# A depthwise convolution split between TensorE and VectorE: 28 of 31 taps on TensorE in place of 24

## What is computed

```python
def conv_module(h, hist, w_pw1, b_pw1, w_dw, b_dw, g_ln, b_ln, w_pw2, b_pw2):
    a = h @ w_pw1 + b_pw1
    u = a[..., :D_MODEL] * jax.nn.sigmoid(a[..., D_MODEL:])
    ext = jnp.concatenate([hist.astype(u.dtype), u], axis=1)
    v = lax.conv_general_dilated(ext, w_dw[:, None, :], (1,), 'VALID',
                                 dimension_numbers=('NWC', 'WIO', 'NWC'),
                                 feature_group_count=D_MODEL) + b_dw
    v = layernorm(v, g_ln, b_ln)
    y = jax.nn.silu(v) @ w_pw2 + b_pw2
    return y, ext[:, -(CONV_WIDTH - 1):]
```

## Time and profile before

| | us |
|---|---|
| median of 3 runs | 1411.05 |
| lowest, highest | 1407.11, 1412.43 |
| the profiled execution | 1407.91 |
| its span in the trace | 1406.1 |
| PE, DVE, ACT, POOL busy | 1358.3, 841.4, 600.8, 728.6 |

### The profile page before, as it was taken

How to read it: one execution, slowest core, us unless ns; L and a number is a source line. 1 busy time by engine, 2 the same in 40 slices (tenths; PEclk the granted TensorE clock), 3 DMA queues, 4 the chain that set the end, 5 groups by cost and what they waited for, 6 DMA issues and landing times.

```text
span 1406.1 us, 26287 instructions
## 1 busy us (share of the span) xinstructions
PE 1358.3 (97%) x11038; PEld 1265.2 (90%) x11038; DVE 841.4 (60%) x1246; ACT 600.8 (43%) x1016; POOL 728.6 (52%) x505
## 2 busy tenths in 40 slices
PE   7899989999999999999999999999999999999997
PEld 7776589999999999999899867768999999999997
DVE  6999666755464544667565665554575454545434
ACT  5112254544444443445555644442364344443432
POOL 3333114488788876333322353430447788887831
PEclk9999979999999999999999999999999999999998
DMA  5443402233322223422111386761222332222221
GB/s 216 136 123 105 149 20 74 88 96 103 103 91 90 91 91 136 150 79 82 46 35 53 123 316 258 275 251 39 66 85 94 104 103 92 90 91 91 90 90 64
DMA packets 106196, 157.52 MB, mean 112 GB/s; under 512 B 7456, under 2 KB 91808, under 8 KB 100832
## 3 DMA queue, kind: packets, MB, share of 16 engines
q1 hardware_dynamic: 98528, 113.35, 25.4%
q0 software_dynamic: 7168, 41.95, 8.0%
q10 hardware_dynamic: 384, 0.55, 0.2%
HBM read 143.07 MB, written 4.03 MB: 105 GB/s over the span
## 4 chain that ended last, share of the span: by engine, by line
PE 85%; DVE 11%; ACT 1%; issue 1%; POOL 1%; DMA 0%; DVEq 0%; SPq 0%; ACTq 0%
PE ps L1627 28%; PE ps L1758 20%; PE ps L1746 18%; PE ps L1888 5%; PE ps L1928 3%; DVE v L1131 3%; PE ps L1977 2%; DVE tap L1118 2%; PE ps L1666 1%; ACT wh L713 1%; PE ps L1679 1%; PE ps L1958 1%; DVE v L1121 1%; POOL wl L573 1%; PE ps L1968 0%
## 5 line engine op out<-in xcount | busy, mean ns | idle before, releaser
L573 POOL TENSOR_TENSOR wl<-raw,wh 128x512 fp32r<-128x512 f32 (+2 forms) x252 | 439.6, 1746 | 475.3 <-ACT wh L713 475.1
L713 ACT ACTIVATE wh<-raw 128x512 fp32r<-128x512 f32 (+2 forms) x253 | 192.6, 762 | 373.5 <-PE ps L1627 190.8
L1627 PE MATMUL ps<-xh,wh 128*128 128x272 f32 x704 | 150.6, 296 | 22.0 <-DVE xl L1059 10.1
L573 POOL TENSOR_TENSOR wl<-wuv,wh 128x512 fp32r<-128x512 f32 x104 | 135.0, 1310 | 49.7 <-ACT wh L713 49.7
L1758 PE MATMUL ps<-mh,wh 128*128 128x272 f32 x768 | 158.6, 288 | 0.0
L1758 PE MATMUL ps<-mh,wl 128*128 128x272 f32 x768 | 158.6, 288 | 0.0
L1758 PE MATMUL ps<-ml,wh 128*128 128x272 f32 x768 | 158.3, 288 | 0.0
L1627 PE MATMUL ps<-xh,wl 128*128 128x272 f32 x704 | 147.6, 292 | 0.0
L1627 PE MATMUL ps<-xl,wh 128*128 128x272 f32 x704 | 147.6, 292 | 0.0
L1627 PEld LDWEIGHTS ps<-xh,wh 128*128 128x128 f32 x704 | 112.8, 193 | 27.3 <-POOL wl L573 15.0
L1758 PEld LDWEIGHTS ps<-ml,wh 128*128 128x128 f32 x768 | 120.4, 188 | 0.0
(11 more groups left out here) (307 smaller groups left out, 3026.0 us busy)
## 6 DMA issues: line engine op xcount, KB each, us to landing
raw<-w_up SPq DMA_DIRECT2D x32, 1024.0 KB, 5.5
raw<-w_down SPq DMA_DIRECT2D x32, 1024.0 KB, 5.2
raw<-w_pw SPq DMA_DIRECT2D x11, 1024.0 KB, 5.2
shifted<-ext SPq DMA_DIRECT2D x112, 66.5 KB, 2.0
raw<-w_o SPq DMA_DIRECT2D x4, 1024.0 KB, 5.5
raw<-w_dq SPq DMA_DIRECT2D x3, 1024.0 KB, 5.3
raw<-w_uq SPq DMA_DIRECT2D x4, 768.0 KB, 4.4
x<-xT SPq DMA_DIRECT2D x4, 544.0 KB, 7.6
```

The costliest lines, as they stand in the source:

```text
L573: pf.tensor_tensor(weight(wl, u), weight_raw(u), f32(weight(wh, u)), ALU.subtract).then_inc(w_lo, 1)
L713: af.activation(weight(wh, u), weight_raw(u), ACT.Copy).then_inc(w_hi, 1)
L1627: m = tf.matmul(ps[:, bank_of(u) + bank, 0:width], w[:, k, :], a[:, k, part], start=(k == 0 and n == 0), stop=(k == nk - 1 and n == 2))
```

## The change

One constant: the taps of the prompt's convolution that TensorE takes in chunks 0 to 6.

```diff
-PE_TAPS = 24
+PE_TAPS = 28
```

## The result

The changed kernel takes 1402.61 us (median of 7 runs, 1398.68 to 1405.43) against 1407.59 us for the kernel before beside it (7 runs). The ratio is 0.995, interval [0.993, 0.997], which is 7.0 us of 1408: it goes with the means of the same runs, 1401.67 and 1408.72 us, while the medians lie 5.0 us apart. Two more sets of runs on other occasions gave 0.9956 [0.9941, 0.9972] and 0.9952 [0.9935, 0.9969]. The profiled execution took 1402.61 us, its span is 1400.8 against 1406.1, so 5.3 us less. The forecast was 1403.9 us and a gain of 7.1 us, with the faster and the same case at nearly even chances, since it lay on the line of 0.5%. The measured ratio lies on that line too.

The account below looks back on a forecast made before the run. VectorE was taken to bound both ends of the convolution stage, TensorE its middle. Gains of 2.7, 0.7, 4.75 and 5.05 us less 6.1 for added steps gave 7.1, so 1411.05 - 7.1 = 1403.9 us, range 1398 to 1410.

Parts of the forecast that it names:

- The step on TensorE: Convolution stage, chunks 0 to 6: one more step of four matmuls each, 0.876 us a step, 6.1 us for seven.
- VectorE's gain in chunk 0: Four L1131 fewer save 3.15 us, less 0.44 us for longer GpSimd diagonals ahead of the residual: 2.7 us.
- Idle place 1: TensorE's wait ahead of chunk 2's first projection, for chunk 1's gate product (L1104): shrinks from 6.1 to 3.4 us.
- Its clock: Chunk 2's two projections, behind the first idle time: lowered TensorE clock loses 1.7 us, bounds 0 and 2.4.
- rival (a): Clock does not fall ahead of chunk 2's first projection: 1.7 us more gain, 1402.2 us; chance 0.21.
- The middle: From chunk 0's tap products to chunk 5's: 92.6 us, no TensorE idle time left, 5.6 us of cover.
- rival (c): VectorE keeps TensorE waiting mid-stage; 2.65 us idle and 1.6 us clock loss stay, gain about 3, 1408 us; chance 0.05.
- T(7): Tap products of chunk 7, T(c) being chunk c's: follow without pause at full clock, ending at 166.2 us against 173.27.
- rival (b): Chunk 7's shifted copies land over 1.8 us later, its tap products wait: gain 4.4 us, 1406.7 us; chance 0.18.
- rival (d): Back-to-back tap products of chunks 5 to 7, 19.3 us, lower the clock: slower, 1423.2 us; chance 0.06.
- The sum at the stage's end: End of chunk 7's tap products: +2.7, +0.7, +4.75, +5.05 and -6.1 us give a gain of 7.1 us.
- moves as a block: Everything behind chunk 7's tap products depends on TensorE or their release, so the 7.1 us gain carries to the end.

Follow-up runs that it names:

- steps 8, 6, 6, 6, 6, 6, 6, 8: Against the changed kernel: TensorE tap steps per chunk, eight in chunks 0 and 7, six between, VectorE taking seven taps in chunks 1 to 6; 1404.85 us, ratio to before 0.9956.

## Why the prediction was right, point by point

- **The step on TensorE**, 0.876 us: 22 steps took 19.02 us, so 0.865; seven fewer steps gave 5.96 us where TensorE was the bound. Right.
- **VectorE's gain in chunk 0**, 2.7 us: L1104 of chunk 1 came at 40.00 in place of 42.32. That execution ran 0.4 us late from the start (L1078 at 24.93 against 24.54), so 2.7. The longer diagonals (1.70 us, as worked out) took their 0.4 us, but not where the prediction had it. The first two L1131 take 3.5 us in both kernels, beside GpSimd's residual; the 0.4 us lie ahead of them, in L1110 (30.27 us, 1.17 us in place of 0.96) and L1129 (34.57 us, 1.83 in place of 1.60), each beside a longer diagonal. So the amount is right. The trace of before also settles what the prediction had only taken for likely, that L1131 waits for the end of the residual: three more of its L1131 take 2.8 to 2.9 us, those of chunks 1 to 3, each beside a residual, for example

```profile
53.45 2.78 DVE v L1131
...
70.55 2.94 DVE v L1131
```

```profile
53.09 2.59 POOL L573 TENSOR_TENSOR wl<-raw,wh 128x1024 fp32r<-128x1024 f32 x1 [4.25 <-ACT wh L713]
...
70.53 2.39 POOL L573 TENSOR_TENSOR wl<-raw,wh 128x1024 fp32r<-128x1024 f32 x1 [5.39 <-ACT wh L713]
```

They end 0.55 and 0.57 us after it, whenever they started. The changed kernel has no such L1131 in chunks 1 to 3, so VectorE is relieved there by 5.2 to 5.3 us a chunk and not by 3.15; that gave nothing more, since TensorE was the bound there.
- **Idle place 1**: 3.40 us, as forecast. **Its clock**: I took 1.7 us lost out of 0 to 2.4. The profiled execution lost none, the second one 1.7, the third none. The prediction treated as one number what is a draw between two; rival (a) had 0.21 and occurred in two of three. That its 1402.2 us lies next to the measured 1402.61 is luck: the stage gained 8.8 us, as it says, and 3.5 of them were lost later.
- **The middle**: T(0) to T(5) 92.40 us against 92.6, with no idle time. Unit 14's residual ended at 127.18 (124.78 + 2.40), T(4) at 133.38: 6.2 us of cover against 5.6. Right; rival (c) did not occur.
- **T(7)** followed with no pause, at full clock: rival (b) did not occur. T(5) to T(7) ran at 1.00 for 19 us, so rival (d) is refuted, too.
- **The sum at the stage's end**: 7.1 us forecast; 8.8, 7.0 and 8.8 us in three profiled executions. The right mechanism.
- **The step that failed** is that behind the stage everything "moves as a block". No changed work lies there, and the lead is still 8.7 us at 676 us, yet 3.5 of 8.8 us went behind it in this pair of executions, at places of lower granted clock in attention and in the last norm. The term missing from the sum is the clock behind the stage. It differs between executions: the shortest span of the changed kernel, 1396.9 us, is 9.2 us below the profiled one of before. It also moved the base: the median of before was 1411.05 in the runs that I had and 1407.59 to this result.
- **The forecast of the time**, 1403.9 us, came within 1.3 us of 1402.61, and that is partly luck: the base was 3.5 us too high and the gain between medians 2.1 us too high. The gain in means, 7.05 us, fits the forecast of 7.1, but as 7.0 to 8.8 us won in the stage less what went later.
- **What stays open**: whether the change makes later falls of the clock more frequent, through where the later waits come to lie. All three profiled executions of the changed kernel have the two new falls in attention and the single one of before has neither, which speaks for it; the mean clocks (0.978 to 0.988 before, 0.983 to 0.989 after) overlap, and more profiles of before were not taken.

## What to carry to other kernels

When work moves between two engines that nearly balance, ask for each piece which engine waits for the other just there; prices don't add, since the same seven steps cost nothing with VectorE loaded and 6 us with it relieved. Read the waits chunk by chunk afterwards and split each chunk by its own bound: one constant for all chunks gave 0.5%, and a list of eight numbers gave 1.0%. Compare such changes at a mark in the trace right behind the stage, where 1 us is visible once a fall of the clock within the stage is allowed for, and not by the total alone, which later falls of the clock move by several.

## What the runs showed of the hardware

- The granted clock fell, or did not, after the same idle time of TensorE. After 3.40 and 3.39 us it stayed, after 3.38 it fell, in one kernel. After 2.67 us in the kernel with steps 8, 6, 6, 6, 6, 6, 6, 8 nothing was lost (130.99 to T(5) at 143.14 is 12.15 us), after 2.65 us in the kernel before 1.6 us were, after 2.97 us some 2.7 us (40.55 to 55.32 is 14.8 us in place of 12.1), after 3.18 us 1.6 us (40.43 to 54.12 is 13.7 us), and ahead of T(7) after 3.25 and 3.38 us 1.5 to 1.7 us (8.5 and 8.7 us in place of 7.0). Idle times of 0.5 to 1.5 us cost none in this stage in any run; 6.1 to 6.5 us cost 2.3 to 2.5 us in each of three executions.
- The Trainium skill (TensorE: Matmul & The Clock Gate, HAM oscillation) warns of long idle gaps of TensorE, which bring the clock back to its lower level. The 6.1 to 6.5 us here agree, and the falls after 2.65 and 2.97 us show that gaps of under half that length can cost clock too, 1.6 and 2.7 us.
- A run of 19 us of tap products with 32-column weights stayed at the 2.4 GHz level (clock 1.00 from 145.5 to 164.4 us of the changed kernel).
- An L1131 (`scalar_tensor_tensor`) that ran beside GpSimd's residual (L573) took 2.7 to 2.9 us in place of 0.76 and ended 0.55 to 0.57 us after it, in all four cases in the kernel before and in the one of the changed kernel (39.19 against 36.08 + 2.55).
